# Expert rows gathered in groups, straight into feature-major form, with h as the stationary operand

## What is computed

```python
def _moe(h, w_rg, b_rg, w_re, b_re, w_gate, w_up, w_down):
    t = h.reshape(B * L, D)
    pg = jax.nn.softmax((t @ w_rg + b_rg).astype(jnp.float32), axis=-1)
    p_top, g_idx = lax.top_k(pg, 1)
    ...
    pe_top, e_idx = lax.top_k(pe, TOP_K_IN_GROUP)
    w = p_top * pe_top / jnp.sum(pe_top, axis=-1, keepdims=True)
    gates = jnp.sum(jax.nn.one_hot(expert_id, N_EXPERTS, dtype=jnp.float32) * w[..., None], axis=1)
    hg = jnp.einsum('td,edf->tef', t, w_gate)
    hu = jnp.einsum('td,edf->tef', t, w_up)
    act = jax.nn.silu(hg) * hu * gates[:, :, None].astype(t.dtype)
    y = jnp.einsum('tef,efd->td', act, w_down)
```

## Time and profile before

| | |
|---|---|
| median of three runs | 1563.26 us |
| profiled execution: its time, and the span from first to last instruction | 1559.05 us, 1557.2 us |
| TensorE busy, mean granted clock | 1428.9 us (92%), 0.959 |
| VectorE, ScalarE, GpSimd busy | 765.3, 323.5, 86.1 us |
| moved by DMA | 436.84 MB, mean 281 GB/s |
| gate/up matmuls L1002 | 1280, 255.1 us |
| down matmuls L1016 | 640, 138.5 us |
| gather matmuls L987 (h_hi and h_lo) | 432, 95.2 and 88.2 us |
| transposes of the gathered rows L995 | 288, 39.4 us |
| expert stages, gate/up of pass 0 to the last | from 272, 487, 1060 and 1391 us, some 120 us each |

### The profile page before, as it was taken

How to read it: one execution, slowest core, us unless ns; L and a number is a source line. 1 busy time by engine, 2 the same in 40 slices (tenths; PEclk the granted TensorE clock), 3 DMA queues, 4 the chain that set the end, 5 groups by cost and what they waited for, 6 DMA issues and landing times. The chain is left out here.

```text
span 1557.2 us, 17818 instructions
## 1 busy us (share of the span) xinstructions
PE 1428.9 (92%) x6473; PEld 738.9 (47%) x6473; DVE 765.3 (49%) x1849; ACT 323.5 (21%) x705; POOL 86.1 (6%) x97
## 2 busy tenths in 40 slices
PE   5998998999678999799999999999998998989985
PEld 3334535444245444456666666454443446454432
DVE  1334205553566544566666666036445455156434
ACT  1104304111223111511111111032112125131101
POOL 0000010000220001000000000010001010100001
PEclk9999999999889999999999999989999999979998
DMA  9989968899895998745555554646998730049995
GB/s 358 386 313 370 387 235 324 344 423 422 328 354 226 417 422 346 271 135 178 177 179 176 180 177 140 230 181 263 420 423 339 292 115 1 27 187 401 424 422 227
DMA packets 152277, 436.84 MB, mean 281 GB/s; under 512 B 6945, under 2 KB 63105, under 8 KB 123137
## 3 DMA queue, kind: packets, MB, share of 16 engines
q1 hardware_dynamic: 136816, 396.93, 66.8%
q10 hardware_dynamic: 11920, 26.24, 4.4%
q0 software_dynamic: 3456, 12.58, 2.3%
HBM read 414.20 MB, written 21.53 MB: 280 GB/s over the span
## 5 line engine op out<-in xcount | busy, mean ns | idle before, releaser
L1002 PE MATMUL bank<-gate_up_weights,hT_gathered 128*64 128x512 f32 (+1 forms) x1280 | 255.1, 598 | 15.4 <-SPq L542 14.3
L840 PE MATMUL bank<-panel,hT 128*128 128x512 f32 x384 | 168.2, 597 | 5.1 <-DVE hT L1241 4.2
L1002 PEld LDWEIGHTS bank<-gate_up_weights,hT_gathered 128*64 128x64 f32 (+1 forms) x1280 | 82.8, 132 | 180.1 <-issue 179.6
L1016 PE MATMUL bank<-down_weights,actT 128*64 128x512 f32 (+1 forms) x640 | 138.5, 603 | 2.5 <-ACT actT L2145 2.5
L1426 DVE SCALAR_TENSOR_TENSOR ada_sums<-panel,cond_columns,ada_sums 128x384 f32<-128x384 f32 x224 | 121.1, 609 | 0.0
L840 PEld LDWEIGHTS bank<-panel,hT 128*128 128x128 f32 x384 | 73.4, 192 | 94.5 <-issue 88.6
L651 PE MATMUL bank<-panel,hT 128*128 128x512 f32 x240 | 107.0, 604 | 3.4 <-DVE hT L1241 2.5
L987 PE MATMUL bank<-h_hi,P 128*128 128x512 f32 x216 | 95.2, 441 | 3.5 <-DVE h_lo L1615 3.5
L987 PE MATMUL bank<-h_lo,P 128*128 128x512 f32 x216 | 88.2, 408 | 0.0
L651 PE MATMUL bank<-panel,oT 128*128 128x512 f32 x192 | 84.3, 595 | 1.3 <-ACT oT L2054 1.3
L2132 ACT ACTIVATE silu<-bank 128x256 f32<-128x256 f32 x36 | 13.9, 385 | 320.0 <-PE bank L1002 320.0
(11 more groups left out here) (330 smaller groups left out, 1923.8 us busy)
## 6 DMA issues: line engine op xcount, KB each, us to landing
gate_up_weights<-in_gate_up_halves SPq DMA_DIRECT2D x148, 1024.0 KB, 13.3
down_weights<-in_down_rows SPq DMA_DIRECT2D x74, 1024.0 KB, 13.5
panel<-in_w_ada SPq DMA_DIRECT2D x27, 2048.0 KB
panel<-in_w_ada SPq DMA_DIRECT2D x16, 1536.0 KB
ada_panel_third<-in_w_ada SPq DMA_DIRECT2D x9, 2048.0 KB
y_by_slot<-y_rows ACTq DMA_DIRECT2D x32, 512.0 KB, 8.1
panel<-in_ret_w_in SPq DMA_DIRECT2D x16, 1024.0 KB
panel<-in_attn_w_qkv SPq DMA_DIRECT2D x5, 2048.0 KB
```

Of the source, the lines that this page charges most:

```text
L840: last = PE.matmul(ps[t][:], hT[:, k, t * 128:(t + 1) * 128], panel[f % 2][:, k, :], start=k == 0, stop=k == KD - 1)
L1002: last = PE.matmul(ps[2][width * s:width * s + width, :], hg[:, j, k, width * s:width * s + width], gu_ring[w][:, 2 * k // KD, :, k % (KD ...
L1016: last = PE.matmul(ps[6 + half][width * s:width * s + width, :], actT[:, c, width * s:width * s + width], dn_ring[w][:, c, half * 512:half ...
```

## The change

Only pass 0 of a layer is still gathered into token rows and turned. Passes 1 and 2 are gathered together, and so are 3 to 5 and 6 to 8. Now a block of h, [128 tokens, 128 features], is the stationary operand and P of two or three passes is moving, 256 or 384 columns, so that the result is feature-major at once. A group has eight k, each of six matmuls (three token tiles, `hhi` and `hlo`): 48 instructions. They are dealt out: 1 and 2 in pass 0; of 3 to 5, two k in pass 1 and six in pass 2; of 6 to 8, one k each in passes 3 and 4 and six in pass 5. Their results alternate between PSUM banks 0, 1, 4 and 5 and are copied straight to `hg`, which has three places now, as P has. Places for passes 3 to 5 are made by VectorE at the start of its part of pass 1, and those for 6 to 8 at that of pass 3; place 2 moves ahead of pass 0. The tables between the passes move: `unit_ranks` in full behind pass 1, `token_slots` and `token_gates` behind 2, `unit_shares` (split off `unit_ranks`) behind 3, `unit_prompts` behind 4. To find room, `lpart` moves from memory of its own to a region that the next mixer's tables use, and `rsm` into P's; hence ScalarE waits for all unit sums of a layer before it issues those tables and before its first Square of the next.

The diff, cut to its core (first memory, then TensorE, what both copying engines share, VectorE from `def row`, and ScalarE at the last `for l`):

```diff
-    Pm = keep("P", [2, TILES, SLOTS], R)
+    Pm = keep("P", [3, TILES, SLOTS], R)
-    lpart = keep("logit_parts", [T])
...
-        return xs_in[:, (0, 2, 1)[t], :] if n % 2 == 0 else xs_mid[:, t, :]
+        return xs_in[:, t, :] if n % 2 == 0 else xs_mid[:, t, :]
...
-    (rsm,), _ = region(("ret_small", [192]), start=small_at)
+    (rsm,), _ = region(("ret_small", [192]), start=place_at)
...
+    (lpart,), _ = region(("logit_parts", [T]), start=mix0 + 2 * size([TILES, D]))
...
-    (hgt, hg), hg_end = region(("h_gathered", [D]), ("hT_gathered", [2, KD, SLOTS]))
+    (hg,), hg_end = region(("hT_gathered", [3, KD, SLOTS]))
+    (hgt,), _ = region(("h_gathered", [D]))
...
+    PLACE_OF = (2, 0, 1, 0, 1, 2, 0, 1, 2)
+    GROUP = {1: (1, 2), 3: (3, 4, 5), 6: (6, 7, 8)}
+    GATHERS, TURNS = 22, 11
+    SPREAD_BANKS = (0, 1, 4, 5)
...
+    def spread_waits(pe, l, count, i):
+        pe.wait_ge(sem(("row_hg_act", "row_hg_dve")[i % 2]), TURNS * l + count)
+
+    def pe_spread(pe, l, first, ks):
+        n = len(GROUP[first])
+        width = n * SLOTS
+        pe.wait_ge(sem("row_P"), ROWS * l + first + n)
+        for k in ks:
+            if first == 1:
+                i, at = k // 2, k % 2 * width
+                if k % 2 == 0 and i < 2:
+                    spread_waits(pe, l, 1, i)
+            else:
+                i, at = k % 4, 0
+                spread_waits(pe, l, {3: 2, 6: 6}[first] + k // 2, i)
+            for t in range(TILES):
+                for part in (hhi, hlo):
+                    last = PE.matmul(ps[SPREAD_BANKS[i]][:, at:at + width], part[:, t, k * 128:(k + 1) * 128],
+                                     Pm[:, 0:n, t, :], start=t == 0 and part is hhi, stop=t == TILES - 1 and part is hlo)
+            if first > 1 or k % 2:
+                last.then_inc(sem("row_gather"), 1)
+
+    def row_turned_wait(pe, l, q, k):
+        if q == 0:
+            if k % 4 == 0:
+                pe.wait_ge(sem(("row_hg_act", "row_hg_dve")[k // 4]), TURNS * l + 1)
+        elif q == 1:
+            if k % 2 == 0:
+                spread_waits(pe, l, 2 + k // 4, k // 2)
+        elif q in GROUP:
+            spread_waits(pe, l, {3: 4, 6: 8}[q] + k // 2, k)
...
         last.then_inc(sem("row_gateup"), 1)
-        if not last_row:
-            pe_row_gather(pe, l, q + 1, 0)
-        else:
+        first, ks = {0: (1, range(0, 4)), 1: (3, range(0, 2)), 2: (3, range(2, 4)), 3: (6, range(0, 1)),
+                     4: (6, range(1, 2)), 5: (6, range(2, 4))}.get(q, (0, ()))
+        if first:
+            pe_spread(pe, l, first, ks)
+        if last_row:
...
         pe_act_T(pe, "row_actT")
-        if not last_row:
-            pe_row_gather(pe, l, q + 1, 1)
+        if q in (0, 2, 5):
+            pe_spread(pe, l, first, range(4, 8) if q == 0 else range(4, 6))
...
             pe_down(pe, half, dn_tiles).then_inc(sem("row_down"), 1)
-            if half == 0 and not last_row:
-                pe_row_T(pe, l, q + 1)
+        if q in (2, 5):
+            pe_spread(pe, l, first, range(6, 8))
...
+    def spread_wait(eng, l, first, k):
+        if first == 1:
+            eng.wait_ge(sem("row_gather"), GATHERS * l + 3 + k)
+            return k
+        eng.wait_ge(sem("row_gather"), GATHERS * l + {3: 7, 6: 15}[first] + k)
+        if k < 2:
+            eng.wait_ge(sem("row_gateup"), ROWS * l + first)
+        return k % 4
...
         def row(l, q):
             n = ROWS * l + q
-            if 1 < q < PAIRS:
-                row_place(l, q + 1)
+            if q in (1, 3):
+                for r in GROUP[{1: 3, 3: 6}[q]]:
+                    row_place(l, r)
...
-            if q < PAIRS:
-                row_gathered(l, q + 1)
+            first = {0: 1, 2: 3, 5: 6}.get(q, 0)
+            if first:
+                spread_copy(l, first, 1)
+                if first > 1:
+                    spread_copy(l, first, 3)
...
+            if first:
+                spread_copy(l, first, 3 if first == 1 else 5)
...
-                if half == 0 and q < PAIRS:
-                    row_turned(l, q + 1)
+            if first > 1:
+                spread_copy(l, first, 7)
...
-            row_turned(l, 0)
+            row_turned(l)
+            row_place(l, 2)
             prompts(l)
...
                 if q == 0:
-                    row_place(l, 2)
                     units(l)
                 elif q == 1:
+                    for t in range(TILES):
+                        unit_ranks(t)
+                elif q == 2:
                     token_slots(l)
                     token_gates()
-                elif q <= TILES + 1:
-                    unit_ranks(q - 2)
-                elif q == TILES + 2:
+                elif q == 3:
+                    for t in range(TILES):
+                        unit_shares(t)
+                elif q == 4:
                     unit_prompts()
...
         for l in range(depth):
+            if l:
+                e.wait_ge(sem("unit_sum"), 2 * TILES * l)
             if l % 3 == 2:
                 e.dma_start(kret[:], A["k_ret"]).then_inc(sem("ret_const"), 16)
```

More of the change, by code:

```diff
@@ L1063, in pe_row @@
                     pe.wait_ge(sem("quad_ready"), 2 * l + 1)
-            last = pe_gateup(pe, q % 2, k, gu_tiles)
+            row_turned_wait(pe, l, q, k)
+            last = pe_gateup(pe, PLACE_OF[q], k, gu_tiles)
             if k == KD // 2 - 1:
@@ L1166, in _, with spread_pair @@
         last.then_inc(sem("vectors_ps"), 1)
+    def spread_wait(eng, l, first, k):
[6 more added lines that the diff above has]
+        return k % 4
+    def spread_pair(first, k, i):
+        bank = ps[SPREAD_BANKS[i]]
+        if first == 1:
+            return (hg[:, 0:2, 2 * k:2 * k + 2, :].rearrange("p j k s -> p k j s"),
+                    bank[:].rearrange("p (k j s) -> p k j s", k=2, j=2))
+        return hg[:, 0:3, k, :], bank[:, 0:3 * SLOTS].rearrange("p (j s) -> p j s", j=3)
     def mod_col(v, k, c):
@@ L1869, in _ @@
             route(l)
-            place(0, rt[:, 192:240].rearrange("p (t e) -> p t e", t=TILES), 0, 2, "row_P", 1)
+            place(PLACE_OF[0], rt[:, 192:240].rearrange("p (t e) -> p t e", t=TILES), 0, 2, "row_P", 1)
             low_part(l, 0, 2)
@@ L2108, in route, with row_gathered, row_turned, spread_copy @@
             S.activation(rt[:, 385:400], rt[:, 370:385], ACT.Exp).then_inc(sem("route_exp"), 1)
[L2110 to L2124 removed]
+        def row_gathered(l):
+            e.wait_ge(sem("row_gather"), GATHERS * l + 1)
+            S.activation(hgt[:, 0:512], ps[0][:], ACT.Copy).then_inc(sem("row_hgt_act"), 1)
+        def row_turned(l):
+            e.wait_ge(sem("row_hT"), 2 * l + 1)
+            S.activation(hg[:, PLACE_OF[0], 0:4, :], ps[0][:].rearrange("p (k s) -> p k s", k=4), ACT.Copy).then_inc(sem("row_hg_act"), 1)
+        def spread_copy(l, first, k):
+            i = spread_wait(e, l, first, k)
+            out, bank = spread_pair(first, k, i)
+            S.activation(out, bank, ACT.Copy).then_inc(sem("row_hg_act"), 1)
         def row(l, q, passes):
@@ L2132, in row @@
             S.activation(silu[:], ps[2][:, 0:FE], ACT.Silu).then_inc(sem("row_silu"), 1)
-            if q < PAIRS:
-                row_gathered(l, q + 1)
-            else:
+            first = {0: 1, 2: 3, 5: 6}.get(q, 0)
+            if first:
+                spread_copy(l, first, 0)
+                if first > 1:
+                    spread_copy(l, first, 2)
+            if q == PAIRS:
                 e.wait_ge(sem("unit_PT"), l + 1)
@@ L2151, in row @@
                 return
-            row_turned(l, q + 1)
+            if first == 1:
+                spread_copy(l, first, 2)
+            elif first:
+                spread_copy(l, first, 4)
+                spread_copy(l, first, 6)
             e.wait_ge(sem("row_y"), 2 * n + 2)
```

76 lines of the change are left out of this document (29 added, 47 removed).

## The result

The changed kernel takes 1579.39 us (median of 4 runs, 1577.90 to 1583.07) against 1563.26. The ratio is 1.0108, 95% interval 1.0089 to 1.0127: slower by 1.1%, some 17 us. The forecast was 1567 with a range up to 1578: the sign of the sum was right, its size was a third of what came, and the time lies 1.4 above the range. Rival (B) had named 1577.

The account below looks back on a forecast made before the run. TensorE was taken to bound the passes of layers 0 to 2 and the loads layer 3. Layer ends -0.7, +2.6, +1.5 and layer 3's loads +2.3 gave +5.7 us on the 1561.2 average: 1567, range 1552 to 1578.

Parts of the forecast that it names:

- Rival (B): Rival, chance 0.2: late requests of passes 1 to 3 pass on to the loads, the chain moves by 6: +16, 1577.
- TensorE's passes: Pass 0 +2.2, pass 1 +1.3, pass 2 +2.6, passes 3 and 4 -2.1, pass 5 +2.6, passes 6 and 7 -2.3 us.
- (C): Rival, chance 0.06: loads of the stationary operand lie bare, 27 a layer if all shows; half is 54 over the kernel, 1615.
- (D): TensorE's 256- and 384-column matmuls cost slightly more or less than 0.126 and 0.179: all by -6 to +5, inside the forecast's range.
- the gathers' term: Gather matmuls behind pass 0's own, one layer: 23.9 us against 24.5, so -0.6.
- TensorE's sum: One layer: -8.2 transposes, -0.6 gathers, +3.9 and +2.0 gaps, +2.5 new wait: -0.4 us.
- the forecast's 0.6: Chance given to the forecast of 1567, of which a fifth lies beyond +7.8 us.
- the wait for P: In pass 1 TensorE stands 2.6 us until VectorE has placed passes 3, 4 and 5; 0.16 there today.
- The loads: Pass 2's down weights asked for 2.2 later move the chain by 2.2; later requests have about 4 us to spare.
- Layer 3's end: The loads end layer 3: +2.2, and 0.1 for stores that get in between, +2.3 us.
- The layers' ends: ScalarE's wait and y gathers 1.5 later: -0.7 from layer 0 to 1, +2.6 from 1 to 2, +1.5 from 2 to 3.
- (A): Rival, chance 0.14: gaps filled, pass 0 no longer, loads not moved; 5.1 a layer in three layers: -14, 1547.

Follow-up runs that it names:

- the places first: The changed kernel with VectorE's places of passes 3 to 5 ahead of the unit tables, and the tables one pass later; alone 1571.88 us, ratio 1.0067.
- down_first: The changed kernel with the second half of pass 0's gathers behind its down matmuls instead of ahead of them; 1582.60 us, ratio 1.0134.
- places_down: The changed kernel with the places first and the second half of pass 0's gathers behind its down matmuls; 1569.06 us, ratio 1.0048.
- after_gathers_behind: The changed kernel with GpSimd's gathers of y waiting until the last pass's extra experts' gate/up weights have landed (layer 3 only); 1578.03 us, ratio 1.0095.
- tables_later: The changed kernel with ScalarE's wait for unit sums and its table loads moved behind the norm's first two Squares and first scaling; 1576.83 us, ratio 1.0095.
- the pair with fewer loads: The kernel before and the changed kernel, each without loading the down weights of passes 2 to 8; 1554.97 us (0.9954) and 1561.97 us (1.0000).
- all_five: The changed kernel with places_down's edits, tables_later's, y_first_inner's and after_gathers_behind's; 1563.17 us, ratio 1.0010 to the kernel before.
- y_first_inner: The changed kernel with VectorE's two multiplies of y ahead of its additions of gathered y, last pass of layers 0 to 2; 1575.48 us, ratio 1.0099.
- all_four: The changed kernel with places_down's edits, tables_later's, and VectorE's multiplies of y ahead of additions in every layer's last pass; 1571.38 us, ratio 1.0060.

## Why the prediction failed, step by step

**TensorE's passes: right.** The 256- and 384-column matmuls start every 0.119 and 0.173 us (0.126 and 0.179 forecast). Pass 0 got 1.8 longer (2.2), pass 2 2.6 (2.6), passes 3 and 4 2.3 shorter (2.1), pass 5 2.6 longer (2.6), 6 and 7 2.4 shorter (2.3); without a fall of the clock the eight passes come to 1.5 us less a layer (0.4 forecast). The waits are 2.61 for P (2.6), 0.94 for act (1.0), 0.47 for actT. The rule of the Trainium skill (page "TensorE: Matmul & The Clock Gate", Part 3) that a weight load overlaps only with another row group, which would have made it 1625, does not hold here: each of these matmuls has its own load of all rows, 0.19 us long, and they start 0.119 and 0.173 apart. (C) is out. (D) came out on its cheap side: 0.007 and 0.006 a matmul, 0.9 us a layer. Two slips of my arithmetic weigh little against this: 23.2 and nine times 0.1 are 24.1 and not 23.9, so that the gathers' term was -0.4 and TensorE's sum -0.2; and a fifth of the forecast's 0.6 is 0.12 where I counted 0.07.

**Pass 1: a term missing.** I had priced the wait for P at its own 2.6 us. In layer 1 TensorE's granted clock fell in it, and in layer 3 1.2 us behind it: the stretch behind the wait in layer 1, and the same one in layer 0:

```profile
517.20:519.20 2.00, 1.99 (x6) 2.00 (x7) 1.48 (x2) 0.00 (x0) 0.00 (x0) 0.50 1.04 438
299.30:301.30 2.00, 2.00 (x11) 2.00 (x12) 1.47 (x2) 0.00 (x0) 0.00 (x0) 1.00 1.01 418
```

At 0.50 (1.2 GHz) six matmuls start where eleven do at 1.00. Pass 1 took 17.6 and 17.5 there, 16.2 in layers 0 and 2, 1.3 more at the worst point: ahead of pass 3's request. It is no accident of one execution: in the six profiled kernels that have this wait (24 layers) pass 1 took 17.4 to 17.7 us in 16 layers and 16.1 to 16.2 in eight; in the four with the places first it took 13.5 to 13.6 in all 16.

**The loads: the step that failed.** It is the sentence that "later requests come up to 6 late, but into a queue that is behind by then (9.9 us from issue to landing at 302), with about 4 us to spare". I took the lag of a request at 302 in the kernel before as slack. But that lag stood on a request at 15.1 us after pass 0; with that one late the queue is shorter at the next, and the next is itself 4.0 later. Of the 4 us of slack less than one was there: by volume the loads are 3.3 behind, not 2.2. That is (B)'s mechanism, in size between it and the forecast. down_first (no better with only the first dry stretch cured, 3.8 behind) and places_down (0.3 behind with both) show it.

**Layer 3's end: a mechanism missing.** I put 0.1 on stores that get in between. The gathers of y get in between too: 1.9 us here by the table, of which after_gathers_behind takes some 1.5 away; in places_down the table's rest is 5.6, which no run took away there. 3.3 + 1.9 make the 5.2 that were 2.3 in my sum.

**The layers' ends: mis-sized.** The gathers of y start 127.0, 127.5 and 126.1 us behind pass 0, where they started at 125.1, 124.1 and 124.4: 1.9, 3.4 and 1.7 later, and I had 1.5. Behind them I had no VectorE queue: the addition of gathered y stands ahead of the multiply that the unit sums need. From layer 1 to 2 the sums end 24.7 us behind the last gate/up, where they ended 18.6 behind it in the earlier trace rows, and ScalarE's wait follows them: I had 2.6 there, 5.0 came, of which tables_later gave 3.1 back. From layer 2 to 3 I had 1.5 and 4.3 came: Square is 4.1 later behind pass 0, only 1.7 of it by the start of the gathers. ScalarE's wait is not the rest, for without it (tables_later) Square stands no nearer, 26.0 behind the last gate/up against 25.5; x itself comes late, and the cause of the other 2.4 stays open. From layer 0 to 1 Square came when it did, counted from pass 0 (142.2, before 142.3), as I had it; but from there to layer 1's pass 0 it takes 75.7 us instead of 72.8. That stretch is pooling. Its inverse counts (issued at 414.72, not 400.15) and modulation weights now share the queue later; and the granted clock is 0.77 in it, where it was 0.86, with TensorE 53.8 us busy instead of 51.2, which is nearly the whole difference. In all nine profiled runs of the changed order with all loads this stretch has a clock of 0.76 to 0.81 and 73.5 to 75.7 us, in the three of the order before 0.84 to 0.86 and 72.5 to 73.2. What lowers the clock there was tested by no run.

**Where the sum ends.** In the medians about 10 of 17 us go with the loads (the pair with fewer loads). The rest is ScalarE's and VectorE's queues at the layers' ends, the extra experts' weights and the clock; how it divides among them is read from traces of single executions and not measured. all_five, which cures five things, is level with the kernel before. It does not show each by itself: tables_later, y_first_inner and after_gathers_behind move the median by 1 to 2 us each, no more than their intervals, and for these the traces carry the verdict. all_five is not faster than before although its passes take 115.9 us a layer instead of 119.1. (A) had 5.1 a layer by that road; but the gathers of y start 125.2, 124.5 and 125.4 us behind pass 0 in layers 0 to 2, where they did before (125.1, 124.1, 124.4). That the loads hold the last store of y there fits the full queue, and no run shows it alone.

## What to carry to other kernels

Where an engine and a load queue run neck and neck, work saved on the engine is worth only what the queue lets through, and the order of the work sets when each buffer comes free: look at every request that comes near a dry stretch, each with the earlier ones already late. The time from issue to landing of one request is no slack for the next. And an engine that becomes quicker calls its own transfers earlier (here, with the places first, the gathers of y), which then stand ahead of the one transfer that is waited for.

## What the runs showed that I had not expected

- A wait of TensorE of 2.61 us was followed by a granted clock of 0.50 for 2 to 3 us in two layers and by 1.00 in the two others, with the same work ahead of it. Over the six kernels with this wait pass 1 was longer by about 1.3 us in 16 of 24 layers. Where the clock fell, 384-column matmuls started every 0.32 us instead of 0.173.
- Asking for one pair of down weights some 3.5 us late in each layer, 20 us ahead of their use, costs 7.7 us in all (before_late_load).
- Indirect gathers of 2 MB issued 4.7 us ahead of the landing of the last weights took nothing from them; issued 12.6 us ahead (all_four against all_five) they took about 3.6.
